# A norm's root moved out of the matmul operand, its scaled operand made inside the attention, halves doubled by DMA, gate results spread over four PSUM pairs

## The reference

```
h = rms_norm(x, norm1_g)                 # x * rsqrt(mean(x^2) + EPS) * g
z = h @ w_in
q, k, v, xr, yr = split(z)               # 512, 128, 128, 512, 512 channels
q = axial_rope(rms_norm(q per head, q_norm_g)) * HEAD_DIM ** -0.5
k = axial_rope(rms_norm(k per head, k_norm_g))
attn = softmax(q k^T) v                  # 8 heads of 64, 2 kv heads
xc = depthwise_conv(xr, 4 taps)
r, i = sigmoid(xc @ block weights) ...   # both directions: four gate products
lru = (h_fwd + h_bwd) * gelu(yr)         # two linear recurrences over the tokens
x = x + concat(attn, lru) @ w_out
```

## Time and profile before

| | us |
|---|---|
| median of 3 runs | 3513.26 (3510.92 to 3513.32) |
| the profiled execution | 3506.94 |
| its span | 3505.1 |
| PE busy | 3364.3 (96%) |
| DVE busy | 2178.6 (62%) |
| ACT busy | 1453.7 (41%) |
| POOL busy | 1118.7 (32%) |
| granted TensorE clock, mean | 0.986 of 2.4 GHz |

### The profile page before, as it was taken

How to read it: one execution, slowest core, us unless ns; L and a number is a source line. 1 busy time by engine, 2 the same in 40 slices (tenths; PEclk the granted TensorE clock), 3 DMA queues, 4 the chain that set the end, 5 groups by cost and what they waited for, 6 DMA issues and landing times.

```text
span 3505.1 us, 44696 instructions
## 1 busy us (share of the span) xinstructions
PE 3364.3 (96%) x16628; PEld 2712.1 (77%) x16628; DVE 2178.6 (62%) x2177; ACT 1453.7 (41%) x1900; POOL 1118.7 (32%) x641
## 2 busy tenths in 40 slices
PE   6999999999999989999999999999899999999997
PEld 4677777888888868888887777777667878888885
DVE  7876868777773456223167888888855564444433
ACT  5687845444441233332233443444452343334113
POOL 1100017888842212111121111111112276675222
PEclk9999999999999999999999999999999999999998
DMA  2000221222252102111111111111122222213322
GB/s 112 25 1 13 67 96 55 78 89 79 83 201 96 48 30 97 36 42 36 36 54 37 43 36 36 42 42 36 42 78 84 78 71 79 90 72 120 142 80 78
DMA packets 55532, 233.04 MB, mean 66 GB/s; under 512 B 6160, under 2 KB 6160, under 8 KB 49680
## 3 DMA queue, kind: packets, MB, share of 16 engines
q1 hardware_dynamic: 55440, 231.78, 18.9%
...
## 4 chain that ended last, share of the span: by engine, by line
PE 81%; DVE 12%; issue 3%; ACT 3%; DMA 0%; POOL 0%; DVEq 0%; SPq 0%; POOLq 0%; ACTq 0%
PE ps L491 44%; PE ps L1334 24%; PE ps L2338 2%; PE ps L2350 2%; PE ps L2327 1%; PE ps L2483 1%; PE ps L2496 1%; PE ps L514 1%; DVE conv_acc L1998 1%; DVE t_wide L977 1%; PE ps L507 1%; PE ps L2435 1%; PE ps L2490 1%; PE ps L2469 1%; DVE small L2038 1%
## 5 line engine op out<-in xcount | busy, mean ns | idle before, releaser
L463 POOL TENSOR_TENSOR w_lo_part<-w_raw,w_hi_part 128x1024 fp32r<-128x1024 f32 x162 | 402.3, 2483 | 1771.6 <-ACT w_hi_part L446 1771.4
L491 PE MATMUL ps<-h_hi_part,w_hi_part 128*128 128x512 f32 x1904 | 621.6, 408 | 45.3 <-DVE h_lo_part L609 28.9
L491 PE MATMUL ps<-h_lo_part,w_hi_part 128*128 128x512 f32 x1904 | 593.3, 393 | 0.0
L491 PE MATMUL ps<-h_hi_part,w_lo_part 128*128 128x512 f32 x1904 | 591.5, 392 | 0.0
L446 ACT ACTIVATE w_hi_part<-w_raw 128x1024 fp32r<-128x1024 f32 x180 | 189.2, 1051 | 742.7 <-PE ps L491 644.2
L491 PEld LDWEIGHTS ps<-h_hi_part,w_hi_part 128*128 128x128 f32 x1904 | 345.9, 190 | 139.9 <-issue 58.9
L491 PEld LDWEIGHTS ps<-h_lo_part,w_hi_part 128*128 128x128 f32 x1904 | 360.8, 190 | 78.1
L491 PEld LDWEIGHTS ps<-h_hi_part,w_lo_part 128*128 128x128 f32 x1904 | 360.2, 189 | 77.9
L1998 DVE SCALAR_TENSOR_TENSOR conv_acc<-u_pad,cols,conv_acc 128x1024 f32<-128x1024 f32 x232 | 307.4, 1325 | 19.4 <-DVE conv_acc L1998 2.8
L1908 DVE TENSOR_TENSOR residual<-residual,ps 128x1024 f32<-128x1024 f32 (+1 forms) x64 | 78.1, 1221 | 282.9 <-PE ps L491 282.8
L491 PE MATMUL ps<-u_lo,w_hi_part 128*128 128x512 f32 x736 | 226.8, 389 | 0.0
...
## 6 DMA issues: line engine op xcount, KB each, us to landing
w_raw<-in_w SPq DMA_DIRECT2D x226, 512.0 KB, 3.5
w_raw_odd<-in_w SPq DMA_DIRECT2D x46, 512.0 KB, 4.1
u_spill<-ffn_u SPq DMA_DIRECT2D x46, 512.0 KB, 3.2
u_wide<-u_spill SPq DMA_DIRECT2D x23, 1024.0 KB, 9.3
residual<-in_x SPq DMA_DIRECT2D x4, 1024.0 KB, 7.9
...
residual<-x_spill SPq DMA_DIRECT2D x4, 1024.0 KB, 5.6
```

Of the source, the lines that this page charges most:

```text
L463: pool.tensor_tensor(WLO[:, slot], WRAW[:, slot], f32(WHI[:, slot]), ALU.subtract).then_inc(w_ready, 1)
L491: last = pe.matmul(PS[:, ps, b * HALF:(b + 1) * HALF], st[:, slot, k, :], at(mv, k, b), start=(k == 0 and n == 0), stop=(k == nk - 1 and n ...
```

## The change

- The weights are reordered: jobs K, V, the first XR, then the four of Q. These seven run on x times the gain only, split at once (`first_hi_act`, `first_lo_dve`), without the root of the first norm.
- K and Q don't need that root; EPS of their norm is instead multiplied by the mean square of the token (tile NEPS), in a new DVE pass (`nr_var_dve`) that reads the sum from slot 3. The rotation (`turn_dve`) now runs ahead of the root, and the gain goes into ACT's copy out of PSUM. V and the first XR are multiplied with the root R0 by one DVE pass each.
- The last Q's rotation and root run on DVE in steps 0 to 7 of the attention.
- K and each Q are copied to both halves of the partitions by four DMAs of 64x1024 (`double`), and their high and low parts are then two passes over 128 partitions in place of four over 64.
- The operand with the root, which the later XR and YR jobs need, is made in steps 11 to 50 of the attention: x is loaded again tile by tile (`again`), DVE scales it in two halves of 128x512 (`scaled_dve`), ACT makes HI (`scaled_hi_act`), DVE makes LO in two halves (`scaled_lo_dve`).
- In the recurrence stage the gates of t = 1 go to slots 2, 3, 0, 1, of t = 2 to 0, 1, 2, 3, of t = 3 to 2, 3, 0, 1, and the XR and YR jobs to slots that fit.

The diff, cut to its core:

```
-J_XR, J_GATE, J_YR = (6, 8, 11, 14), (7, 10, 13, 16), (9, 12, 15, 17)
+J_V, J_Q = 1, 3
+J_XR, J_GATE, J_YR = (2, 8, 11, 14), (7, 10, 13, 16), (9, 12, 15, 17)
...
+        R0, NY0, NTMP0 = (scratch(f"first_{c}", [P, S], F32, t) for c, t in (("rstd", 19), ("y", 7), ("a", 6)))
+        XS = [scratch(f"x_again{i}", [P, S], F32, 4 + i) for i in range(2)]
+        NTURN = scratch("qk_turned", [P, S], F32, 1)
+        DUP = [[scratch(f"both_halves{n}{i}", [P, S], F32, t) for i, t in enumerate(ts)]
+               for n, ts in enumerate(((4, 5), (0, 7), (0, 1), (1, 2), (1, 6)))]
+        NEPS = xyt("qk_eps", [P, S], F32, 6)
...
+        XR_SLOT, YR_SLOT = (0, 0, 2, 0), (1, 3, 1, 2)
+        GATE_SLOT = (2, 3, 2, 3), (2, 3, 0, 1), (0, 1, 2, 3), (2, 3, 0, 1)
...
+        def first_hi_act(act, k):
+            act.activation(HI[:, k, :], X[:, k, :], ACT.Copy, scale=col("norm1_g", k)).then_inc(h_hi, 1)
+        def first_lo_dve(dve, k):
+            dve.wait_ge(h_hi, 8 * GEN_NORM1 + k + 1)
+            dve.scalar_tensor_tensor(LO[:, k, :], X[:, k, :], col("norm1_g", k), f32(HI[:, k, :]), ALU.mult,
+                                     ALU.subtract).then_inc(h_ready, 1)
+        def scaled_dve(dve, k, half):
+            cols = slice(HALF * half, HALF * half + HALF)
+            if half == 0:
+                dve.wait_ge(x_part[k % 4], 16 * (2 + k // 4))
+            ins = dve.scalar_tensor_tensor(XS[k % 2][:, cols], XS[k % 2][:, cols], col("norm1_g", k), R0[:, cols],
+                                           ALU.mult, ALU.mult)
+            if half:
+                ins.then_inc(hn_ready, 1)
+        def scaled_hi_act(act, k):
+            act.wait_ge(job_done, J_Q + 4)
+            act.wait_ge(hn_ready, HN_BASE[0] + k + 1)
+            act.activation(HI[:, k, :], XS[k % 2][:, :], ACT.Copy).then_inc(h_hi, 1)
...
+            act.activation(dst[:, :], psl(slot), ACT.Copy, scale=col(gain)).then_inc(ps_free[slot], 1)
+        def nr_root_act(act, steps, idx):
+            v, y = N2[idx % 2], N3[idx % 2]
+            act.wait_ge(nv_ready, idx + 1)
             if idx > 1:
                 act.wait_ge(rope_ready, idx - 1)
-            rsqrt_act(act, steps, 2, HD, N2[idx % 2][:, :], N3[idx % 2][:, :], ny_ready)
-        def nr_dve(dve, steps, j, idx, dst, gain):
+            steps.do(act.activation(y[:, :], v[:, :], ACT.Ln))
+            act.activation(y[:, :], y[:, :], ACT.Exp, scale=-0.5).then_inc(ny_ready, 1)
...
+            if part == 0:
+                dve.wait_ge(ps_free[j % 2], j // 2 + 1)
+                dve.tensor_tensor(NTURN[:, :], dst[:, :], ROPE[:, 0, :], ALU.mult)
+            elif part == 1:
+                steps.do(dve.stream_shuffle(N4[:, :], dst[:, :], [(i + 16) % 32 for i in range(32)]))
+            elif part == 2:
+                steps.do(dve.tensor_tensor(N4[:, :], N4[:, :], ROPE[:, 1, :], ALU.mult))
+            else:
+                steps.do(dve.tensor_tensor(dst[:, :], NTURN[:, :], N4[:, :], ALU.add))
+        def nr_var_dve(dve, idx):
+            dve.wait_ge(nsum_done, idx + 1)
+            dve.scalar_tensor_tensor(N2[idx % 2][:, :], psl(3), 1.0 / HD, NEPS[:, :], ALU.mult, ALU.add
+                                     ).then_inc(nv_ready, 1)
+        def nr_dve(dve, steps, idx, dst):
             v, y = N2[idx % 2], N3[idx % 2]
             dve.wait_ge(ny_ready, idx + 1)
-            dve.wait_ge(ps_free[j % 2], j // 2 + 1)
             rsqrt_dve(dve, steps, v[:, :], y[:, :], N4[:, :])
-            steps.do(dve.scalar_tensor_tensor(dst[:, :], dst[:, :], col(gain), v[:, :], ALU.mult, ALU.mult))
-            dve.tensor_tensor(v[:, :], dst[:, :], ROPE[:, 0, :], ALU.mult)
-            steps.do(dve.stream_shuffle(N4[:, :], dst[:, :], [(i + 16) % 32 for i in range(32)]))
-            steps.do(dve.tensor_tensor(y[:, :], N4[:, :], ROPE[:, 1, :], ALU.mult))
-            dve.tensor_tensor(dst[:, :], v[:, :], y[:, :], ALU.add).then_inc(rope_ready, 1)
+            dve.tensor_tensor(dst[:, :], dst[:, :], v[:, :], ALU.mult).then_inc(rope_ready, 1)
+        def project_dve(dve, steps, j, idx, dst):
+            for part in range(4):
+                turn_dve(dve, steps, j, dst, part)
+            nr_var_dve(dve, idx)
+            nr_dve(dve, steps, idx, dst)
         def nr_pe(pe, idx):
             def mid():
                 pe.wait_ge(nsq_ready, idx + 1)
-                sum_all(pe, 2, N1, True, True, con("ones_head")).then_inc(nsum_done, 1)
+                if idx:
+                    pe.wait_ge(nv_ready, idx)
+                sum_all(pe, 3, N1, True, True, con("ones_head")).then_inc(nsum_done, 1)
...
+        def double(sp, src, n):
+            for t in range(2):
+                for half in range(2):
+                    sp.dma_start(DUP[n][t][64 * half:64 * half + 64, :], src[64 * t:64 * t + 64, :]).then_inc(doubled, 16)
...
+            double(sp, KF, 0)
+            for j in range(5, 8):
+                load(sp, j, j % 2)
+            sp.wait_ge(rope_ready, 2)
+            sp.wait_ge(k_lo, 2)
+            double(sp, QF[0], 1)
...
+            sp.wait_ge(q_lo, 2)
+            again(0)
+            sp.wait_ge(rope_ready, 5)
+            double(sp, QF[1], 2)
+            sp.wait_ge(q_lo, 4)
+            again(1)
+            sp.wait_ge(vt_done, 1)
+            double(sp, QF[2], 3)
+            for k in range(2, KT):
+                sp.wait_ge(h_ready, 8 * GEN_SCALED + k - 1)
+                again(k)
+                if k == 4:
+                    sp.wait_ge(q_lo, 6)
+                    double(sp, QF[3], 4)
...
+                if g == 1:
+                    nr_root_act(act, st, 4)
+                if a < 3 and n in (8, 9):
+                    q_hi_act(act, a + 1, n - 8)
+                if 13 <= g < 53 and g % 5 == 3:
+                    scaled_hi_act(act, g // 5 - 2)
...
+            act.wait_ge(sq_ready, KT)
+            nr_read_act(act, 0, 0, KF, "k_norm_g")
             split_act(act, 1, 0)
-            act.wait_ge(h_ready, 8)
-            nr_act(act, st, 0, 0, KF)
+            act.wait_ge(ss_sum, 1)
+            act.activation(NEPS[:, :], psl(2), ACT.Identity, bias=small(EPS2), scale=EPS / D).then_inc(eps_row, 1)
+            nr_root_act(act, st, 0)
+            rsqrt_act(act, st, 2, D, R0[:, :], NY0[:, :], y0_ready)
...
+                if g < 4:
+                    turn_dve(dve, st, J_Q + 3, QF[3], g)
...
+                elif g == 7:
+                    dve.tensor_tensor(QF[3][:, :], QF[3][:, :], v[:, :], ALU.mult).then_inc(rope_ready, 1)
+                if a < 3 and n in (9, 10):
+                    q_lo_dve(dve, a + 1, n - 9)
+                k = (g - 11) // 5
+                if 11 <= g < 51 and g % 5 in (1, 2):
+                    scaled_dve(dve, k, g % 5 - 1)
+                if 14 <= g < 51 and g % 5 == 4:
+                    scaled_lo_dve(dve, k, 0)
+                if 15 <= g < 51 and g % 5 == 0:
+                    scaled_lo_dve(dve, k, 1)
...
+            for k in range(4):
+                first_lo_dve(dve, k)
+            square_dve(dve, 0, 1)
+            for k in range(4, 6):
+                first_lo_dve(dve, k)
+            square_dve(dve, 0, 2)
+            for k in range(6, KT):
+                first_lo_dve(dve, k)
+            for k in range(3, KT):
+                square_dve(dve, 0, k)
+            dve.wait_ge(rope_in, 32)
+            for part in range(4):
+                turn_dve(dve, st, 0, KF, part)
+            dve.wait_ge(eps_row, 1)
+            nr_var_dve(dve, 0)
+            nr_dve(dve, st, 0, KF)
+            dve.wait_ge(y0_ready, 1)
+            rsqrt_dve(dve, st, R0[:, :], NY0[:, :], NTMP0[:, :])
...
+            project_dve(dve, st, J_Q, 1, QF[0])
+            for part in range(4):
+                turn_dve(dve, st, J_Q + 1, QF[1], part)
+            for i in range(2):
...
+            elif t == 0 or m < 2:
+                pe.wait_ge(gate_evac, 4 * t + m - 1)
+            elif m == 2:
+                pe.wait_ge(ps_free[0], 4 + t)
             else:
-                pe.wait_ge(gate_evac, 4 * t + m - 1)
-            three_pass(pe, 2 + m % 2, WHI[:, j % 2, m, :], WLO[:, j % 2, m, :], XCH, XCL
+                pe.wait_ge(y_evac, t)
+            three_pass(pe, GATE_SLOT[t][m], WHI[:, j % 2, m, :], WLO[:, j % 2, m, :], XCH, XCL
...
-            pe.wait_ge(k_lo, 4)
-            pe.wait_ge(ny_ready, 5)
+            pe.wait_ge(k_lo, 2)
+            pe.wait_ge(y0_ready, 1)
             scores(0)
-            scores(1)
-            job(pe, J_XR[0] // 2, J_XR[0] % 2)
+            nr_pe(pe, 4)()
             pe.wait_ge(ps_free[1], 3)
+            pe.wait_ge(r_applied, 1)
             for k in range(QT):
                 mm = pe.transpose(PS[:, 1, k * P:k * P + P], VF[:, k * P:k * P + P], con("ident"))
             mm.then_inc(vt_done, 1)
+            pe.wait_ge(nv_ready, 5)
+            scores(1)
...
+            job(pe, 0, 0, h_gen=GEN_NORM1)
+            job(pe, 0, 1, ks=range(0, 3))
+            pe.wait_ge(rope_in, 32)
+            nr_pe(pe, 0)()
```

(64 more changed lines are left out.)

168 lines of the change are left out of this document (82 added, 86 removed).

## The result

| | before | after |
|---|---|---|
| median | 3511.75 (7 runs, 3507.31 to 3513.37) | 3521.04 (7 runs, 3517.20 to 3524.07) |
| span of the profiled execution | 3505.1 | 3521.6 |
| PE / DVE / ACT busy | 3364.3 / 2178.6 / 1453.7 | 3372.1 / 2182.1 / 1443.6 |

After takes 1.0029 of the time of before (95% interval 1.0020 to 1.0039, or 7 to 14 us): by the medians 9.3 us **slower**, where 15.5 us faster was forecast.

A forecast was written before the change was run, and what follows sets the result against it. DVE was taken to set the pace at the start, PE in the attention, with DVE near its limit in the recurrence. Terms 15.8 - 2.5 - 3.4 + 5.6 = 15.5 us off 3513.26 gave 3497.8, range 3489 to 3508.

The forecast's parts named there:

- a half-width pass: Attention from step 11: a DVE pass of 0.75 us fits into 0.85 us of spare time, costing nothing.
- ACT gets one pass of 1.06 in five steps: Attention: ACT's added high part of the scaled operand fits into 0.7 us of spare time, costing nothing.
- forecast 5.9: Attention, steps 0 to 63: the change gives back 2.5 us in the first steps and 3.4 us later.
- The rival: Attention: DVE becomes the bound; half passes waiting about 1 us for high part or x tile give 3525 us; chance 0.06.
- the two pairs of steps with Q's low parts: Steps 25, 26, 41, 42: half-width pass meets a full low part of q; PE loses 1.6 us per pair.
- signs of being wrong: ACT waiting over 1 us for a DMA before q's high part; row maxima late in steps 11 to 50; step 0 beyond 130.
- Steps 0 to 7: Early attention: one more full DVE pass makes each step 3.36 us against 2.94, giving back 2.5 us.
- The start: Up to step 0 of the attention: turned at 123.2 us instead of 139.03, 15.8 us won.
- POOL's hits: Start: DVE passes slowed by POOL's weight work, 2.1 us each, five and a half-sized one counted from 30 us on.
- The doubling: Start: copying K or a Q to both partition halves takes 5.0 us; the first Q's is covered but for 0.1.
- The rival of 7.9 us: Start: each doubling is slow, 2.9 us more, twice on the chain; gain 9.7, time 3503.6; chance 0.15.
- The recurrence stage: After the attention: new PSUM slots spare gate 2 its wait for gate 0's read, 5.6 us won.

The follow-up runs named there:

- experiment 1: The changed kernel with ACT's high parts of the scaled x one attention step earlier: 3512.68 us, ratio 1.0005 to the kernel before.
- experiment 2: The changed kernel with DVE's low parts of Q one attention step later: 3510.19 us, ratio 0.9995 to the kernel before.
- both moves: The changed kernel with ACT's high parts of x one step earlier and DVE's low parts of Q one step later: 3498.71 us, ratio 0.9963.
- experiment 5: The kernel with both moves, with gates, XR and YR back in the PSUM slots of the kernel before: 3502.63 us, ratio 0.9982.

## Why the prediction was wrong

**The attention: the step that failed.** The prediction said "From step 11 on a half-width pass (...) fits into the 0.85 us of the earlier trace rows: no cost" and "ACT gets one pass of 1.06 in five steps, with 0.7 to spare: nothing". As the kernel was ordered, both failed: the attention cost 29.7 us more, forecast 5.9. What these sums of durations left out is who waits for whom. A pass of DVE that needs one of ACT costs the time until ACT comes to it, and ACT comes to it only behind a copy that needs PE's turn and an exponential that needs DVE's row maximum. The rival had it nearly in these words ("a half pass that waits about 1 us for its high part"), with its result "slower", and got a chance of 0.06 because "ACT's high part is one step ahead". One step ahead in g is not one step ahead in time: ACT's step g ends with the exponential of g + 2, for which DVE has to reach step g + 1. Writing ACT's and DVE's queues side by side for steps 13 to 15 should have shown it. Of the 23.6 us, 7.9 were the x tiles' (experiment 1: seven turns, late by 0.7 to 1.7 us) and 14.4 Q's low parts' (experiment 2), which the rival didn't name: there a full pass of DVE and one of ACT come in each of two steps running, and the ring takes 5.2 us a step. The remaining 1.3 comes only with both moves: most of it is the eighth x tile's, whose turn (step 45) is on time in after, behind the late turns of Q's pair, and 1.1 us late when only Q's passes are moved.

That the attention with both moves costs 6.1 us, forecast 5.9, is in part luck. Steps 8 to 63 lose 3.2 us of it, forecast 3.4, but the two pairs of steps with Q's low parts, forecast at 3.2, lose 1.0 and 0.3, and steps 10 to 12, forecast at 0.2, lose 1.7.

Two of the prediction's signs of being wrong were seen: row maxima late in steps 11 to 50, and ACT waiting for a DMA ahead of the high part of q (11.05 us). The second tells little: by the forecast's own times ACT would have waited there too, for a copy that ended at 86.7.

**Steps 0 to 7.** Step 8 is turned at 151.50, 25.1 us behind step 0, against 22.2 before (161.2 - 139.03): 2.9 given back, forecast 2.5. The sum is right, but the even spacing of 3.36 us wasn't seen: steps 1 to 8 took 3.39, 2.33, 4.04, 2.92, 2.94, 3.10, 3.25 and 3.13 us. DVE's extra pass cost little. Some 1.1 us are step 1, behind a turn at the low level (1.88 us), and 1.1 are step 3, where PE waited for ACT's copy:

```profile
136.16 1.06 PE L2494 MATMUL ps<-con,prob 128*128 128x128 f32 x8 [1.04 <-ACT prob_t L1543]
```

That copy stood in ACT's queue behind the two passes of the last Q's root (to 135.11), for which the forecast had no term on ACT.

**The start.** 12.6 us instead of 15.8. The steps came in the order told. POOL's hits from 30 us on took 11.1 us together, forecast 11.5, though two of the six fell on other passes than counted. The doubling was mis-sized: 6.7 to 6.8 us, not 5.0. It left DVE idle for 2.2 us at K and 3.1 at the first Q, where the forecast had it covered but for 0.1. The rival of 7.9 us was too high. The 7.3 us that the prediction worked out from the Trainium skill ("SBUF — State Buffer", "Door 1: The DMA port swizzle") came nearest, but it probably counts the fixed time twice: that section gives 196 GB/s as measured at 1 MiB, beside a higher asymptote. Part of the loss was hidden by an error the other way: the scores of step 1, forecast at the low level and 2.6 us, took 1.0 us. PE's first job began at 13.5, forecast 12.3, and PE waited for ACT's squares 6.6 and 4.0 us, forecast 5 and 3.

**The recurrence stage.** 6.0 us, forecast 5.6, and the prediction's waits of YR jobs for weights came (4.5 us, three times). But only 4.2 to 4.4 of it are the rotation, to which the forecast put all; the rest is the clock, which fell at one place in the trace of before and not in that of after (experiment 5). That the sum fits so well is luck.

**The level.** 27 runs of the kernel before in one comparison have a median of 3510.89, against the 3513.26 of the three runs that the forecast started from. So its base was high, by 1.5 us against the median of the seven runs (3511.75), which makes the miss of the time (3521.04 - 3497.8 = 23.2 us) look smaller than the miss of the change (9.3 + 15.5 = 24.8 us). The traces differ by 16.5 us, but only by 11.1 at the reload. The part behind it, unchanged code, takes 3505.1 - 461.54 = 3043.6 us in the trace of before and 3048.9 in that of after; the other kernels of this study have 3044.6 to 3049.1 there, whether their front is of the one kind or the other. It is spread from run to run, and the trace of before is below all of them.
